# GpSimd's share of the weight low parts in the index stage, and where the last branch's input is split

## The reference

```python
for l in range(DEPTH):                       # first block
    h = rms_norm(x, mix_pre_norm[l])
    proj = h @ w_in[l]                       # qkv, z, a, b, retention q k v g, pool, three gates
    y = (gt[:, :, 0] * (o_dn @ w_branch_dn)  # gated delta rule
         + gt[:, :, 1] * (o_pool @ w_branch_pool)
         + gt[:, :, 2] * (o_ret @ w_branch_ret))   # chunkwise retention
    x = x + rms_norm(y @ w_out, mix_post_norm[l])
    x = x + rms_norm(swiglu(rms_norm(x, ffn_pre_norm[l])), ffn_post_norm[l])
...
def block(t0):                               # second block, branch a, 128 queries at a time
    rel = relu(einsum('bqhd,bsd->bqhs', iqb, ik) * idx_scale)
    score = einsum('bqh,bqhs->bqs', iwb, rel)
    _, idx = lax.top_k(where(causal, score, -inf), 64)
    ...                                      # attention over the 64 keys found
```

## Time and profile before

| what | us |
|---|---|
| median of 3 runs | 1971.97 (1971.37 to 1972.77) |
| the profiled execution | 1979.08 |
| its span, first to last instruction | 1977.3 |
| TensorE matmul busy | 1906.6 (96%) |
| VectorE busy | 1260.3 (64%) |
| ScalarE busy | 969.9 (49%) |
| GpSimd busy | 335.6 (17%) |
| mean granted TensorE clock | 0.985 |

### The profile page before, as it was taken

The page is one execution under the profiler, slowest core; times in us unless marked ns, Lnnn a source line. Parts: engine busy times, 40 slices in busy tenths (PEclk is TensorE's granted clock), DMA queues, the critical chain, the costliest instruction groups (busy, mean ns, idle before and its releaser), DMA issues.

```text
span 1977.3 us, 35114 instructions
## 1 busy us (share of the span) xinstructions
PE 1906.6 (96%) x14820; PEld 1817.9 (92%) x14820; DVE 1260.3 (64%) x1647; ACT 969.9 (49%) x1395; POOL 335.6 (17%) x184
## 2 busy tenths in 40 slices
PE   7989999999999999999999989999999989999998
PEld 7989998998888999989988889999999889999997
DVE  6874467665579545767647775576646694567743
ACT  5634355544463434554445444655534434656642
POOL 1061121000013402300001342220000243220000
PEclk9999999999999999999999999999999999999999
DMA  5433344656444333555565553345655654345662
GB/s 208 163 122 107 118 144 144 212 185 193 138 140 151 106 107 123 168 168 195 195 199 171 190 171 118 128 150 194 191 184 169 205 181 134 129 149 182 193 199 100
DMA packets 91580, 317.50 MB, mean 161 GB/s; under 512 B 11552, under 2 KB 12704, under 8 KB 91040
## 3 DMA queue, kind: packets, MB, share of 16 engines
q1 hardware_dynamic: 91424, 315.26, 48.8%
HBM read 304.99 MB, written 1.05 MB: 155 GB/s over the span
## 4 chain that ended last, share of the span: by engine, by line
PE 83%; DVE 10%; ACT 3%; issue 2%; POOL 1%; DMA 0%; SPq 0%; ACTq 0%; DVEq 0%
PE bank L1864 82%; DVE wlo L1056 3%; DVE area L1062 3%; DVE area L1056 2%; ACT whi L623 1%; ACT area L617 1%; PE bank L2301 1%; PE bank L2043 1%; DVE xT L1062 0%; DVE area L1522 0%; DVE area L1520 0%; DMA raw<-in_weights 0%; POOL area L1650 0%; ACT L610 0%; POOL wlo L1650 0%
## 5 line engine op out<-in xcount | busy, mean ns | idle before, releaser
L1056 DVE TENSOR_TENSOR wlo<-raw,whi 128x1024 fp32r<-128x1024 f32 x512 | 674.6, 1331 | 454.3 <-ACT whi L623 453.6
L1864 PE MATMUL bank<-hh,whi 128*128 128x256 f32 x2928 | 839.7, 287 | 43.6 <-DVE wlo L1056 18.3
L1864 PE MATMUL bank<-hl,whi 128*128 128x256 f32 x2928 | 822.5, 281 | 0.0
L1864 PE MATMUL bank<-hh,wlo 128*128 128x256 f32 x2928 | 822.0, 281 | 0.0
L623 ACT CAST whi<-raw 128x1024 fp32r<-128x1024 f32 x572 | 588.7, 1046 | 419.6 <-PE bank L1864 391.6
L1864 PEld LDWEIGHTS bank<-hh,whi 128*128 128x128 f32 x2928 | 561.0, 192 | 59.9 <-issue 26.9
L1864 PEld LDWEIGHTS bank<-hl,whi 128*128 128x128 f32 x2928 | 559.1, 191 | 1.5 <-issue 1.4
L1864 PEld LDWEIGHTS bank<-hh,wlo 128*128 128x128 f32 x2928 | 558.4, 191 | 0.0
L1650 POOL TENSOR_TENSOR area<-area 128x512 f32<-128x512 f32 (+4 forms) x90 | 137.9, 1539 | 855.6 <-ACT area L617 684.7
L1864 PE MATMUL bank<-area 128*128 128x128 f32 (+5 forms) x1544 | 203.0, 291 | 9.9 <-issue 9.2
L1650 POOL TENSOR_TENSOR wlo<-raw,whi 128x1024 fp32r<-128x1024 f32 x60 | 149.2, 2487 | 346.0 <-ACT whi L623 345.7
(11 more groups left out here) (124 smaller groups left out, 1946.9 us busy)
## 6 DMA issues: line engine op xcount, KB each, us to landing
raw<-in_weights SPq DMA_DIRECT2D x572, 512.0 KB, 3.5
area<-area SPq DMA_DIRECT2D x96, 64.0 KB, 3.8
area<-area SPq DMA_DIRECT2D x16, 128.0 KB, 4.0
cst<-in_const SPq DMA_DIRECT2D x1, 1188.0 KB, 10.2
cst<-in_const SPq DMA_DIRECT2D x1, 1024.5 KB, 8.0
xT<-in_x SPq DMA_DIRECT2D x4, 256.0 KB, 5.8
out<-xT SPq DMA_DIRECT2D x1, 1024.0 KB, 3.8
area<-in_lev SPq DMA_DIRECT2D x2, 384.0 KB, 8.1
```

The source lines that it names most:

```text
L1056: return v.tensor_tensor(dst, x, y, op)
L1864: return e.matmul(ps, x, y, start=start, stop=stop, skip_group_check=skip)
```

## The change

Two edits. First, `SHARED` for layers 2 and 3 starts from other chunks: 315, 316, 317, 322, 323, 324 and then 326, 328, ... 356, 22 in all as before. GpSimd no longer splits 314, 318 and 320; VectorE does. GpSimd splits 315, 317 and 323 in VectorE's place. Second, in layers 0 and 1 ScalarE and VectorE run two more steps of `fill` (57 and 58) after retention, ahead of the high and low part of wret's input.

```diff
 SHARED = {146 * L + c for L in (0, 1) for c in (4, 8, 12, 51, 54, 57, 60, 63)}
-SHARED |= {292 + 140 * L + c for L in (0, 1) for c in range(22, 66, 2)}
+
+SHARED |= {314 + 140 * L + c for L in (0, 1) for c in chain((1, 2, 3, 8, 9, 10), range(12, 44, 2))}
@@ in scalar, first(L)
                 run(retention(L), fill)
+                next(fill, None)
+                next(fill, None)
 
                 a.wait_ge(*proj.at("wdn", L, 6))
                 branch_high("wret", L, *v_ret.at("out", L))
```

## The result

| | before | after |
|---|---|---|
| median of the runs | 1971.67 (4 runs, 1964.4 to 1972.77) | 1951.3 (4 runs, 1945.07 to 1956.54) |
| ratio, 95% interval | | 0.9886 [0.9859, 0.9914] |
| profiled execution | 1979.08 | 1948.02 |
| its span | 1977.3 | 1946.2 |
| mean granted clock | 0.985 | 0.989 |

By the ratio the change takes 22.5 us off (17.0 to 27.8), by the medians 20.4; 24.0 us off were forecast. In the code of after the lines of before stand a few further down: the split and the other subtractions of VectorE are L1059 (were L1056), its score steps L1065, ScalarE's cast L624, GpSimd's operations L1655, TensorE's matmuls L1869, MAX8 L1525 and MATCH_REPLACE8 L1527.

The account below looks back on a forecast made before the run. TensorE, busy in 96% of the span, bounds the kernel, so only its waits and slow clock count: 15.1 us (index stages) + 8.9 us (end of retention) = 24.0 us off, giving 1948.0 us, range 1942 to 1958.

Parts of the forecast that it names:

- The sum: Whole kernel: 15.1 us from the index stages plus 8.9 us from the end of retention, 24.0 us off.
- Part 1, the second half: Index stage, second score to chunk 321: the 5.98 us wait and 1.8 us of clock go, 0.8 us stays.
- Part 1, the first half: Index stage, first half's score and top-k rounds: the 0.61 us wait goes, at cost zero.
- 2.6 us of cover: Index stage: 318 and 319 done by 1129.7, while the second score cannot start before ScalarE's relus at 1132.3.
- Part 2: End of retention, layers 0 and 1: the 2.77 us wait at chunk 60 and 1.7 us of clock go; twice, 8.9 us.
- A: Rival, end of retention: GpSimd goes ahead of VectorE's split of 62, 1.9 us late; 1951.8 to 1955.2; chance 0.17.
- B: Rival, index stage: one more GpSimd instruction ahead of split 320 or 321, 2.4 us and 1.7 of clock; 1956.2; chance 0.09.
- C: Rival: gain given back at the bank of columns 8 and 9, swaps or first attention round; 1956 or 1965; chance 0.07.
- up to 2 us a stage: Index stage, behind chunk 321: allowance for chunk 323's bank, swaps, fetches and casts, itself costed at nothing.
- D: Rival, index stage: three GpSimd splits in a row stop the top-k rounds; 1974, or 1983 without part 2's gain; chance 0.03.
- E: Rival: the change does not do what it says, a chunk falls into another step; waits stay, 1972; chance 0.02.

Follow-up runs that it names:

- part 1 alone: Kernel before with only GpSimd's new index-stage chunks, without the two fill steps after retention: 1953.62 us, ratio 0.9918.
- one of the halves alone: Kernel before with only the first half's chunks moved (GpSimd 315, 316, 317, then 320, 322, 324 as before): one run, 1969.79 us.
- the run of the part alone: Kernel before with only the two fill steps after retention, old chunks for GpSimd: 1956.57 us, ratio 0.9934.
- rerun: The whole change measured again, three times, against the kernel before: 1945.22 (ratio 0.987), 1952.05 (0.9878) and 1941.53 us (0.9851).
- the version beyond the change: Whole change plus GpSimd's delta-rule query product and start of pooling one step later in layers 0 and 1: 1941.1 and 1945.96 us, 0.9843 and 0.9861 against before.

## Why the prediction was right

**The sum.** 24.0 us was forecast; four comparisons gave 22.5, 25.6, 24.1 and 29.4 us, and the waits and the clock of the profiles 24.8.

**Part 1, the second half.** Counted from the start of the second score, the forecast's timeline and the one of after:

| | forecast | after |
|---|---|---|
| score ends | 5.1 | 5.2 |
| split of 320 done, GpSimd's 322 starts | 6.3 | 6.3 |
| split of 321 done | 9.8 | 9.8 |
| bank emptied | 11.1 | 11.0 |
| TensorE ready for it | 10.4 | 10.8 |
| wait | 0.8 | 0.40 |

Which instructions would meet was right, down to the one add in the score and the half microsecond that the split of 321 loses (1.72 against 1.22). The mis-sized term is when TensorE arrives: the score starts 0.4 us earlier relative to it than I took. It is worth 0.8 us in two layers. Layer 3 waits as long, but its split of 321 takes 2.28 us.

**Part 1, the first half.** I had costed it at zero with 2.6 us of cover. That holds in the time: the 0.61 us wait is gone and nothing new came in the first half. But one collision was missed, the mask behind the top-k rounds, one operand wide (VectorE, layer 2; the same in layer 3):

```profile
1111.14 1.32 DVE L1062 TENSOR_SCALAR area<-area 128x128 f32<-128x128 f32 x1
...
1559.71 0.22 DVE L1062 TENSOR_SCALAR area<-area 128x128 f32<-128x128 f32 x1
```

The first ran beside GpSimd's add of 1110.75 and took 1.1 us more. So not only two operands in SBUF are held up; the prediction named the two-port mode beside them, but its working went by two operands alone. The Trainium skill (SBUF — State Buffer, Who interferes with whom) has this case: tensor_scalar can enter a two-port mode and then needs the pair; the 1.32 us agree. The cover took it up. In the second half there is less cover: the mask of step 322 took 1.17 us in after and 1.12 us in part 1 alone, and there it helped to make the wait of 1.23 us at chunk 325.

That the first half costs nothing by itself was right. That it also decides the phase of the second half was not seen: one of the halves alone gave 2.81 us where I had left 5.98. The forecast did not rest on it, as its timeline was that of both halves together. For one half alone my way of adding would have failed: I expected 1 us of the first half, and its waits give 2 x (0.61 + 5.98 - 2.81) = 7.6 us.

**Part 2.** Every step came in the forecast order: casts of 60 and 61 ahead of the product, GpSimd's 60 ahead of the retention steps, which pay 2.2 us (2.4 forecast), then evacuation, 61, the low part of the input, 62. The forecast was 8.9 us; the run of the part alone gave 13.0 (8.5 to 17.5). The waits and the clock that its trace has at this place are the 8.9; the excess lies inside the interval and has no cause that was shown.

**The rivals.** A, that GpSimd goes ahead of VectorE's split of 62: VectorE began it at 280.67, GpSimd's 63 arrived at 281.00, 0.33 us later (0.3 forecast), and waited. It was close, and the order of arrival decided, as by the rule of the Trainium skill cited in the prediction. B, a real stall of 3 us at chunk 321: 0.40 and 0.61 us in four traces. C, the gain given back: in small it came, at a bank that the prediction did not cost. It looked at chunk 323; late was the evacuation of step 322 behind the mask, for chunk 325, by 0.50 to 0.65 us in one layer of each rerun, nothing in after, and 1.23 us in part 1 alone. That is inside the "up to 2 us a stage" that the prediction allowed, and the clock stayed at 1.00 behind it. In the version beyond the change the waiting was given back nearly whole, 12 us further on. D, the top-k rounds stopped: MAX8 and MATCH_REPLACE8 kept 0.29 and 0.28 us beside three splits in a row. (Its price was added up short: 4.1 + 3 + 3 + 3 x 1.7 is 15.2 us, not 14; the rival did not come.) E: the chunks fell where they should.

## What to carry to other kernels

When a second engine takes a share of element-wise work, place it beside instructions of the first that it does not hold up in a trace, such as MAX8 and MATCH_REPLACE8 here, and not beside those with two operands in SBUF (nor beside the mask above, with one); three splits in the score instead of in the top-k rounds behind it cost some 15 us here (1.4 against 16.1 us off, each with an interval of 4 to 5 us). Ahead of a wait in an in-order queue, put what the critical engine needs next: two steps moved past one wait were worth 9 to 13 us. And ask what is late next before trusting a gain: where the next wait is nearly as long, only some clock can be won, and the clock may fall there too.

## What the runs showed of the hardware beyond what was expected

**Which waits cost clock.** All waits of TensorE over 1 us in the fourteen traces of this case but the first of each, by length, and whether the granted clock fell to the lower level (1.2 GHz) during the wait or within 2 us behind it:

| wait, us | fell | stayed at 1.00 |
|---|---|---|
| 1.06 to 1.74 | 0 | 111 |
| 1.93 (4 us behind one of 1.3) | 2 | 2 |
| 2.33 to 2.44 | 15 | 13 |
| 2.76 to 5.99 | 55 | 0 |

Each of the middle rows is one place of the program, in its two layers. Here the wait of 2.34 us at 1295.17 in before, and that of 2.34 us at 1272.43 in after (windows of before, then of after):

```profile
1297.00:1300.00 3.00, 3.00 (x17) 3.00 (x17) 1.29 (x2) 0.19 (x1) 0.00 (x0) 0.55 0.31 85
```

```profile
1272.50:1275.00 2.50, 2.50 (x22) 2.50 (x23) 2.47 (x3) 0.00 (x0) 1.20 (x1) 1.00 0.66 210
```

So bringing a wait from 2.8 to 1.7 us saves 1.7 us more than its length in this kernel, and a wait near 2.4 us costs that in 15 of 28 cases. The lower clock also comes at places without such a wait (185.9 to 190 in after, where the window shows 0.50), which this table leaves out.

**TensorE has two paces at the full granted clock.** The windows from 380 to 440 us, where TensorE never waits, of before, of after and of the whole change's first rerun:

```profile
380.00:440.00 60.00, 60.00 (x512) 60.00 (x511) 40.24 (x55) 27.11 (x43) 0.00 (x0) 1.00 0.58 188
```

```profile
380.00:440.00 60.00, 60.00 (x532) 60.00 (x531) 40.34 (x56) 28.80 (x44) 0.00 (x0) 1.00 0.60 194
```

```profile
380.00:440.00 60.00, 60.00 (x512) 60.00 (x511) 39.94 (x55) 26.86 (x44) 0.00 (x0) 1.00 0.57 187
```

The instructions are the same, the clock is 1.00, and 512 or 532 matmuls fit into 60 us: they start 0.1178 or 0.1133 us apart. The first rerun is the program of after and has the pace of before, so it is not the change. Within an execution the pace turns now and then and then holds, here for 100 us. Adding up the long stretches at the slower pace gives 413 us in the profile of before, 311 in after, and 257, 393 and 51 in the three reruns; at 3.8% of them that is 16, 12, 10, 15 and 2 us. Taken off the spans (1977.3, 1946.2, 1947.3, 1956.7, 1937.3) it leaves 1961.6 for before and 1934.4 to 1941.8 for the change, 1937 in the mean: 24 us apart. So it narrows the spread of the four profiles of the change from 19 to 7 us, and gives some 4 of the 31 us between the two first profiles; with 17.9 us of waits and 4.5 of clock, about 5 us of them stay unexplained. These sums are estimates: what counts as a long stretch was my choice. With the same correction the version beyond the change (154 and 161 us of slower pace, spans 1935.5 and 1936.3) comes to 1930, 7 us under the whole change, and the lower clock cost it 13.7 and 10.2 us in all while TensorE worked, against 18.2 in the mean of the four; this rests on two profiles. What sets the pace and what turns it stays open; no run here was made for it.
